# Neighbourhood attention: the values of four head pairs by seven block products, and two small moves in the layer after it

## The reference, cut to what matters

```
def na_mixer(h, hc, w_qkv, rpb, w_o, need_ctx):      # h: latent tokens, hc: context tokens, 256 each
    q = project_q(h)                                 # h @ w_qkv[:, :1024]
    k, v = project_kv(h)                             # h @ w_qkv[:, 1024:]
    kc, vc = project_kv(hc)
    y = neighbourhood_attention(q, k, v, kc, vc, rpb).reshape(B, S, H * d) @ w_o
```

## Time and profile before

| | |
|---|---|
| median of three runs | 1903.69 us (1902.11 to 1905.91) |
| profiled execution | 1905.67 us, span 1903.8 us |
| TensorE busy (PE) | 1743.9 us, 92% of the span; granted clock 0.969 in the mean |
| VectorE busy (DVE) | 915.2 us, 48% |
| ScalarE busy (ACT) | 367.5 us, 19% |
| DMA | 395.77 MB, mean 208 GB/s |
| chain that ended last | PE 78%, DMA 18%, DVE 3% |

### The profile page before, as it was taken

The page is one execution under the profiler, slowest core; times in us unless marked ns, Lnnn a source line. Parts: engine busy times, 40 slices in busy tenths (PEclk is TensorE's granted clock), DMA queues, the critical chain, the costliest instruction groups (busy, mean ns, idle before and its releaser), DMA issues.

```text
span 1903.8 us, 33559 instructions
## 1 busy us (share of the span) xinstructions
PE 1743.9 (92%) x14306; PEld 1374.2 (72%) x14306; DVE 915.2 (48%) x1948; ACT 367.5 (19%) x872; POOL 0.2 (0%) x4
## 2 busy tenths in 40 slices
PE   8999999999999999999999999999999866666765
PEld 4455687888888886777888888788888655445554
DVE  1488878666666426677544412478433211111112
ACT  0343413221110114222211102203412100000001
POOL 0000000000000000000000000000000000000000
PEclk9999999999999999999999999999999988888888
DMA  9523342222222116445243533313296999999997
GB/s 382 205 112 143 125 177 89 89 84 82 82 100 95 65 61 219 165 165 196 91 169 140 222 153 133 133 67 133 89 377 249 426 428 429 428 429 428 429 427 298
DMA packets 32947, 395.77 MB, mean 208 GB/s; under 512 B 3664, under 2 KB 6736, under 8 KB 9040
## 3 DMA queue, kind: packets, MB, share of 16 engines
q1 hardware_dynamic: 32848, 394.33, 51.8%
HBM read 393.26 MB, written 1.05 MB: 207 GB/s over the span
## 4 chain that ended last, share of the span: by engine, by line
PE 78%; DMA 18%; DVE 3%; issue 1%; ACT 1%; SPq 0%; DVEq 0%
PE bank L600 24%; PE bank L1880 13%; DMA arena<-w_moe 10%; PE bank L1589 8%; DMA ring<-w_moe 7%; PE bank L653 5%; PE bank L3349 3%; PE bank L2093 3%; PE bank L898 2%; PE bank L2089 1%; PE bank L1199 1%; PE bank L807 1%; PE bank L2449 1%; PE bank L1175 1%; PE bank L3360 1%; PE bank L2145 1%
## 5 line engine op out<-in xcount | busy, mean ns | idle before, releaser
L600 PE MATMUL bank<-layer_input,ring 128*128 128x256 f32 x1152 | 255.3, 382 | 0.0
L600 PEld LDWEIGHTS bank<-layer_input,ring 128*128 128x128 f32 x1152 | 219.2, 192 | 31.9 <-issue 2.6
L3349 PE MATMUL bank<-arena 128*32 128x128 f32 x2008 | 79.8, 325 | 51.6 <-DMA arena<-w_moe 51.4
L1589 PE MATMUL bank<-arena,ring 128*128 128x256 f32 x544 | 121.8, 380 | 0.5 <-DMA ring<-w_ffn_out 0.5
L3501 DVE TENSOR_TENSOR arena<-arena,bank 128x128 f32<-128x128 f32 x32 | 9.2, 287 | 223.0 <-PE bank L3349 223.0
L1880 PE MATMUL bank<-arena 128*128 128x256 f32 x504 | 115.7, 379 | 0.0
L3349 PEld LDWEIGHTS bank<-arena 128*32 128x32 f32 x2008 | 69.1, 131 | 63.0 <-DMA arena<-w_moe 61.2
L1589 PEld LDWEIGHTS bank<-arena,ring 128*128 128x128 f32 x544 | 103.2, 190 | 15.1 <-DMA ring<-w_ffn_out 0.9
L1880 PEld LDWEIGHTS bank<-arena 128*128 128x128 f32 x504 | 95.8, 190 | 13.0 <-DVE arena L2009 0.2
L653 PE MATMUL bank<-arena,ring 128*128 128x256 f32 x452 | 99.1, 380 | 0.8 <-DVE arena L2252 0.6
L653 PEld LDWEIGHTS bank<-arena,ring 128*128 128x128 f32 x452 | 85.7, 190 | 13.2 <-issue 1.0
(11 more groups left out here) (505 smaller groups left out, 2667.4 us busy)
## 6 DMA issues: line engine op xcount, KB each, us to landing
arena<-w_moe SPq DMA_DIRECT2D x45, 2048.0 KB, 25.8
ring<-w_moe SPq DMA_DIRECT2D x45, 2048.0 KB, 26.5
ring<-w_ffn_in SPq DMA_DIRECT2D x22, 2048.0 KB, 7.7
ring<-w_ffn_out SPq DMA_DIRECT2D x8, 2816.0 KB, 9.9
ring<-w_proj SPq DMA_DIRECT2D x7, 3072.0 KB, 9.9
ring<-w_ada_late SPq DMA_DIRECT2D x8, 2560.0 KB, 9.0
ring<-w_na_pair SPq DMA_DIRECT2D x8, 1536.0 KB, 6.2
arena<-w_far SPq DMA_DIRECT2D x11, 1024.0 KB, 6.7
```

What stands on the lines that cost most here:

```text
L600: last = pe.matmul(out, a, b, start=(k == 0), stop=(k == len(lhs) - 1))
L1589: last = eng.matmul(out, w[:, k * P:(k + 1) * P], x[:, k, :], start=(start and k == 0), stop=(stop and k == half - 1), skip_group_check=True)
L3349: ins = eng.matmul(bank[x][group[q], 0:P], xe[:, k, SLOTS * e:SLOTS * e + SLOTS], weight(e, first, last, (x * KT + k) * FE + q * P, P), st ...
```

## The change

**Values by seven products.** The values of four pairs are made at once, in two groups (g = 0 for pairs 0 to 3, g = 1 for pairs 4 to 7). For a group the tokens (halved into context and latent) times the weights (channels halved, output columns halved) are a 2 x 2 block product. It is computed by seven block products in place of eight, in the form with sums made beforehand: four sums of token halves (`s1` to `s4`, once, for both groups), four of weight halves (`t1` to `t4`, per group, in the ring's own slot), all made by VectorE with one operation of 128 x 1024 each. A block product for one half i of 128 tokens is four matmuls of 128 x 128 weights with 256 columns; there are 7 x 2 x 2 = 28 of them. ScalarE takes five intermediate results per (g, i) out of PSUM (`snap`, 128 x 256), and VectorE adds three per (g, i) (`cross`, two; `far_right`, one).

**Stream.** The pairs' chunks are six of 2048 KB: queries and keys of pairs 0 and 1, values of group 0, queries and keys of 2 and 3, values of group 1, queries and keys of 4 and 5, and of 6 and 7. The biases are kept for 8 heads at a time, and those of heads 8 to 15 are loaded in two parts during turns 1 and 3. The far tiles come one by one (512 KB) into two buffers, 32 loads.

```diff
-FAR_BUFFERS, FAR_EACH = 3, 2
-FAR_PER_PAIR = (0, 4, 4, 4, 5, 5, 5, 5)
+FAR_BUFFERS, FAR_EACH = 2, 1
+FAR_PER_PAIR = (8, 1, 5, 6, 6, 3, 3, 0)
...
-          ("na_pair", NA_PAIRS, 3072), ("na_o", 2, 4096),
+          ("na_pair", 6, 4096), ("na_o", 2, 4096),
...
         i, used = FAR_BUFFERS, 0
+        values_done = {0: VALUE_STEPS, 4: 2 * VALUE_STEPS}
         for u in range(NA_PAIRS):
-            if u + RING < NA_PAIRS:
-                sp.wait_ge(self.sem("na_proj_done"), u + 1)
-                load(u + RING, (g0 + u) % 2, g0 + u + RING)
+            if u == 0:
+                sp.wait_ge(self.sem("na_qk_done"), 4)
+                load(2, g0 % 2, g0 + 2)
+            if u in (1, 3):
+                sp.wait_ge(self.sem("na_biased"), 8 if u == 1 else 16)
+                heads = slice(0, 4) if u == 1 else slice(4, 8)
+                self.load_biases(sp, 8, heads, self.rest_in)
             used += FAR_PER_PAIR[u]
-            while i < min(FAR_LOADS, used // FAR_EACH + FAR_BUFFERS):
+            while i < min(FAR_LOADS, used):
                 self.load_far(sp, i)
                 i += 1
+            if u in values_done:
+                sp.wait_ge(self.sem("products_done"), NA_VALUES["products_done"] + values_done[u])
+                load(3 if u == 0 else 5, (g0 + 1) % 2, g0 + (3 if u == 0 else 5))
+            if u == 2:
+                sp.wait_ge(self.sem("na_qk_done"), 8)
+                load(4, g0 % 2, g0 + 4)
+            while i < min(FAR_LOADS, used + FAR_BUFFERS):
+                self.load_far(sp, i)
+                i += 1
...
-        sp.wait_ge(self.phase_done, self.merged)
+        sp.wait_ge(self.mixed, KT)
...
+        def value(g, i, n):
+            w, at = self.na_value_weights(g), self.na_steps(g, i)
+            near, far = slice(i * P, i * P + P), slice(CTX + i * P, CTX + i * P + P)
+            low, high, far_high = self.A[:, 0:4, near], self.A[:, 4:8, near], self.A[:, 4:8, far]
+            s1, s2, s3, s4 = [x[:, :, near] for x in v["sums"]]
+            x, y, out, start = {1: (low, "lo0", left, True), 2: (high, "hi0", first_cross, True),
+                                3: (s1, "t1", second_cross, True), 4: (s2, "t2", left, False),
+                                5: (s4, "hi1", second_cross, False), 6: (s3, "t3", left, False),
+                                7: (far_high, "t4", left, False)}[n]
+            if (i, n) == (0, 1):
+                self.na_value_loaded(pe, g)
+            if n in (3, 4, 5, 6, 7):
+                pe.wait_ge(s["vector_in"], ready + ((0, 0, 0, 2, 4, 6, 7, 8), (0, 0, 0, 9, 10, 10, 11, 12))[g][n])
+            if n == 1 and (g, i) != (0, 0):
+                pe.wait_ge(s["scalar_out"], at["free"])
+            if n == 2 and (g, i) != (0, 0):
+                pe.wait_ge(s["vector_out"], at["pair_free"])
+            if n in (4, 5, 6, 7):
+                pe.wait_ge(s["scalar_out"], at[{4: "first", 5: "fifth", 6: "second", 7: "third"}[n]])
+            for k in range(4):
+                last = pe.matmul(out, x[:, k, :], w[y][:, k * CTX:(k + 1) * CTX], start=(start and k == 0), stop=(k == 3),
+                                 skip_group_check=True)
+            last.then_inc(s["products_done"], 1)
...
+        def weight_sum(g, n, count):
+            w = self.na_value_weights(g)
+            if n == 1:
+                self.na_value_loaded(dve, g)
+            if n == 4:
+                dve.wait_ge(s["products_done"], self.na_value_done(g, 1, 2))
+            x, y = {1: ("lo1", "lo0"), 2: ("hi1", "t1"), 3: ("hi1", "lo1"), 4: ("hi0", "t2")}[n]
+            add(w[f"t{n}"], w[x], w[y], ALU.subtract, count)
+        def cross(g, i):
+            at, home = self.na_steps(g, i), self.na_value_homes(v, g, i)
+            dve.wait_ge(s["products_done"], self.na_value_done(g, i, 5))
+            dve.wait_ge(s["scalar_out"], at["second"])
+            if g == 1:
+                dve.wait_ge(s["o_done"], 2)
+            dve.tensor_tensor(home["c11"], bank[7][:, 0:CTX], v["first"], ALU.add).then_inc(s["vector_out"], 1)
+            dve.tensor_tensor(home["c12"], bank[7][:, CTX:2 * CTX], v["second"], ALU.add).then_inc(s["vector_out"], 1)
+        def far_right(g, i):
+            at, home = self.na_steps(g, i), self.na_value_homes(v, g, i)
+            dve.wait_ge(s["scalar_out"], at["third"])
+            dve.tensor_tensor(home["c22"], v["third"], v["fifth"], ALU.add).then_inc(s["vector_out"], 1)
...
         dve.wait_ge(s["squared"], at["squared"] + KT)
-        dve.memset(v["blk"], 0.0).then_inc(s["cmp_steps"], 1)
...
-        for n in range(6):
+        for n in range(4):
+            evict(n)
+        dve.memset(v["blk"], 0.0).then_inc(s["cmp_steps"], 1)
+        for n in (4, 5):
             evict(n)
...
-        self.phase_end(eng, who)
...
-            link(dve.tensor_tensor(mixed[:, oc, :], mixed[:, oc, :], other, ALU.add))
+            dve.tensor_tensor(mixed[:, oc, :], mixed[:, oc, :], other, ALU.add).then_inc(self.mixed, 1)
...
+            if oc == 0:
+                pe.wait_ge(self.sem("branch_used"), KT - 1)
+            for k in range(KT):
+                if oc == 0:
+                    pe.wait_ge(self.mixed, k + 1)
+                w = ((oc % 4) * KT + k) * P
+                last = pe.matmul(bank[oc % 2][:, 0:LAT], self.w_out_chunk(oc // 4)[:, w:w + P], mixed[:, k, :],
+                                 start=(k == 0), stop=(k == KT - 1))
+            last.then_inc(s["y_ready"], 1)
```

More of the change, by code:

```diff
@@ new lines, in queries @@
+        def queries(u, lo=0, hi=KT):
+            if lo == 0:
+                pe.wait_ge(s["q_copied"], u)
+            for k in range(lo, hi):
+                last = query(u, k)
+            if hi == KT:
+                last.then_inc(s["qk_done"], 1)
+        left, first_cross, second_cross = bank[2][:, 0:CTX], bank[7][:, 0:CTX], bank[7][:, CTX:2 * CTX]
+        ready = NA_VALUES["vector_in"]
+        def value(g, i, n):
[21 more added lines that the diff above has]
+            last.then_inc(s["products_done"], 1)
@@ new lines, in na_heads_dve, with add @@
+        ready_0 = NA_VALUES["vector_in"]
+        A = [[self.A[:, 4 * y:4 * y + 4, c:c + CTX] for y in range(2)] for c in (0, CTX)]
+        s1, s2, s3, s4 = v["sums"]
+        def add(out, x, y, op, count):
+            dve.tensor_tensor(out, x, y, op).then_inc(ready, 1)
+            dve.wait_ge(ready, ready_0 + count)
+        def weight_sum(g, n, count):
[6 more added lines that the diff above has]
+            add(w[f"t{n}"], w[x], w[y], ALU.subtract, count)
@@ new lines, in na_heads_dve @@
+        maxima(0)
+        weight_sum(0, 3, 5)
+        add(s4, A[0][1], s2, ALU.subtract, 6)
+        add(s3, A[0][0], A[1][0], ALU.subtract, 7)
+        normalize(0)
+        cross(0, 0)
+        fars(0, 0, 1)
+        queries(1)
+        weight_sum(0, 4, 8)
+        fars(0, 1, 2)
+        turned(0)
+        far_right(0, 0)
+        fars(0, 2, 4)
+        cross(0, 1)
+        fars(0, 4, 6)
+        far_right(0, 1)
+        fars(0, 6, 8)
+        attended(0)
+        maxima(1)
+        weight_sum(1, 1, 9)
@@ new lines, in na_heads_dve @@
+        normalize(1)
+        weight_sum(1, 2, 10)
+        turned(1)
+        weight_sum(1, 3, 11)
+        queries(2)
+        fars(1, 0, 1)
+        attended(1)
+        maxima(2)
+        normalize(2)
+        cross(1, 0)
+        fars(2, 0, 2)
+        turned(2)
+        fars(2, 2, 3)
+        queries(3)
+        weight_sum(1, 4, 12)
+        fars(2, 3, 5)
+        attended(2)
+        maxima(3)
+        normalize(3)
+        fars(3, 0, 3)
+        turned(3)
+        far_right(1, 0)
+        fars(3, 3, 4)
@@ L2242, in na_heads_dve @@
+        queries(4)
+        fars(3, 4, 6)
+        attended(3)
+        maxima(4)
+        normalize(4)
+        cross(1, 1)
+        fars(4, 0, 3)
+        turned(4)
+        far_right(1, 1)
+        fars(4, 3, 4)
+        queries(5)
+        fars(4, 4, 6)
+        attended(4)
+        for u in (5, 6):
             maxima(u)
             normalize(u)
-            for i in range(min(FAR_PER_PAIR[u], 4)):
-                far(sum(FAR_PER_PAIR[:u]) + i)
-            self.na_turned(u, 0, s, v, dve, dve.tensor_copy, "pt_dve")
@@ L2247, in na_heads_dve @@
-            if FAR_PER_PAIR[u] > 4:
-                far(sum(FAR_PER_PAIR[:u]) + 4)
-            if u + 1 < NA_PAIRS:
-                queries(u + 1)
-            dve.wait_ge(s["o_done"], u + 1)
-            dve.tensor_copy(v["oT"][:, u * LAT:(u + 1) * LAT], bank[6][:, 0:LAT]).then_inc(s["o_used"], 1)
+            fars(u, 0, 2)
+            turned(u)
+            fars(u, 2, 3)
+            queries(u + 1)
+            attended(u)
+        maxima(7)
+        normalize(7)
+        turned(7)
+        attended(7)
```

289 lines of the change are left out of this document (206 added, 83 removed).

## The result

| | before | after |
|---|---|---|
| median | 1902.9 us (4 runs) | 1911.07 us (4 runs, 1909.52 to 1912.65) |
| ratio | | 1.0038, 95% interval 1.0026 to 1.005 |
| profiled execution | 1905.67 us, span 1903.8 | 1909.74 us, span 1908.0 |
| TensorE / VectorE busy | 1743.9 / 915.2 us | 1740.3 / 933.3 us |
| last copy of the attention output | 907.60 | 919.14 |

The changed kernel is slower by about 0.4%. The forecast was 1905.2 with a range of 1896.0 to 1911.5: the time lies at the upper end of the range, and the size is nearer to that of rival (b), two far buffers as the bound, than to the forecast.

What follows compares the result with a forecast made beforehand. TensorE was taken to bound the kernel up to the experts, DMA among them. Attention +3.9, clearing -1.0 and merge -1.4 gave +1.5 us: 1907.2 against the profiled execution, 1905.2 against the median of 1903.69; range 1896 to 1911.5.

Steps and rivals of the forecast that it cites:

- rival (b): Attention stage: two far buffers set the pace; at 4.5 us per load instead of 3.5, +9.1 us, 1912.8; chance 0.25.
- TensorE relieved by 10.3 us: Values in the attention stage: 28 block products of 1.73 us, 48.4 us, replace 58.7 us of TensorE work.
- rival (c): Values: 256-column records run at the pace of two of 128, a product takes 1.83 us; +2.2 on the forecast, 1907.4; chance 0.05.
- Turn 0 without a wait: First attention turn: VectorE's sums come in time for TensorE's products, `s4` at 740.8, wanted at 741.7, cover 0.9 us.
- Two buffers late for the far tiles: Turns 2 to 4: end of a tile to start of the one after next takes 3.5 us, tiles 0.9 to 3.5 late.
- The chunks behind far loads: Key chunks for turns 4 and 5 and pairs 6 and 7 queue behind far loads 13 and 25, issued 807.9 and 857.9.
- the walk: Turn-by-turn estimate of the attention stage's output copies, from 789.9 in turn 1 to the last at 911.5, 3.9 us later than before.
- TensorE could begin `keys(4)` at 813.1 and waits 2.9: Turn 3: the keys' chunk lands at 816, so TensorE waits 2.9 us, then keys take 6.87.
- Turn 1: VectorE, copy to copy, takes 16.9 us, including 0.5 for ScalarE's snapshot ahead of the exponentials; TensorE's list is 15.9.
- The last turn: End of the attention stage: attention ends 14.4 us after the previous copy instead of 19.1; output weights may be 1.5 late.
- Clearing and merge: Second block: moving the `memset` from ahead of the sums gains 1.0 us, projection starting directly behind the branches gains 1.4.
- Its point of decision, 3.8 us: Rival (b): the kernel is slower by over 3.8 us from a far load of 3.8 us on.

Runs made afterwards that it cites:

- the version with the filler: Changed kernel with four single far buffers, plus eight 128x128 products of constants ahead of the last turn's transposes: 1900.41 us, ratio 0.998 to the kernel before.
- The fillers: Changed kernel with unused products of constants where TensorE stood in turns 3 and 5, two far buffers kept: 1908.3 us, ratio 1.0022 to the kernel before.

## Why the prediction was right in direction and short in size

The forecast had the change 1.5 us slower, and by the medians it is 8.2. The range held the result, but in part by luck: its upper end had been drawn for loads of up to 4.3 us, and what came instead was a clock that fell and two smaller terms.

**TensorE relieved by 10.3 us: right.** Products come every 1.73 us (738.16 to 743.34 for three, in the version with the filler), so rival (c) falls.

**Turn 0 without a wait: right,** 57.8 against 57.7 us.

**Two buffers late for the far tiles: right, and a little under.** From the end of a tile to the start of the one after next it is 3.64 and 3.90 us in turn 2 and 3.89 in turn 4 (3.6 to 3.9 in the seven waits of turns 2 to 6), of which the load itself is 3.47, for the first, and 3.72, for the third; I took 3.5 in all. So the landing was at most 0.4 us over the middle value, well under the 4.5 us of rival (b). Turn 2's miss of 0.6 us is this. The Trainium skill ("DMA: Bandwidth & Descriptors", Anatomy of one DMA) would give an estimate of 3.2 for the load; the measured ones are above it. The fit there is measured on transfers that GpSimd issues, which the prediction did not say, and these are issued on SyncE.

**The chunks behind far loads: right.** Issued at 809.1 and 862.6, landed 8.25 and 8.56 us later; the walk had 807.9 and 857.9, and 8.1 and 7.9. With four buffers both waits shrink to 1.06 and 0.28.

**What the waits cost: wrong, and this is the main miss.** The step "TensorE could begin `keys(4)` at 813.1 and waits 2.9" took a wait to cost its own length and the work after it 6.87 us. The work after it ran at half the clock: 2.8 us more in turn 3, 1.5 in turn 5. The fillers show it. Of the 8.1 us by which the stage missed its forecast 4.4 stand in these two rows, and 3.3 came back at the stage's end when the fillers took them away.

**Turn 1: 1.3 us short, by ScalarE.** Turn 1 is 18.2 us with two buffers and with four, and with the far tiles halved, so it is neither loads nor far tiles. The walk had counted 0.5 for ScalarE's snapshot ahead of the exponentials. The rows show more (the first two of the changed kernel, the last of the kernel before):

```profile
780.04 0.37 ACT L2528 COPY extra<-bank 128x256 f32<-128x256 f32 x1 [8.64 <-PE bank L2187]
780.43 1.28 ACT L2515 ACT_TABLE_LOAD   x1
...
746.86 1.28 ACT L2275 ACT_TABLE_LOAD   x1
```

The snapshot waits for TensorE's product until 780.04, 0.4 us after the negated maximum is there, and behind it stands a table load, which ScalarE makes before the first exponential after the silu. In the kernel before it stood directly behind the silu, nine microseconds before the exponentials of turn 1 could start, and cost nothing. Now the exponentials start at 781.73 instead of 779.7, and TensorE waits 0.69 and 0.25 for probabilities and 0.44 for a sum. No run here moved that load, so this is read from the rows and not tested.

**The other turns.** Some 1.8 us are left over the other turns, 0.8 of it in turn 5, where the chunk took 8.56 us to land for the walk's 7.9.

**The last turn: right,** 14.6 us against 14.4, with the output weights 1.52 us late under its hole.

**Clearing and merge: near.** Forecast 1.0 and 1.4. The clearing is worth 1.1 between two traces that both keep the clock (212.5 and 211.5, before rounding), the merge 1.7. The 3.2 beyond, in the profile of before, are the clock again.

**The balance.** Stage +12.0, clearing -4.3, merge -1.7, the start and the stretches without a change -1.8: +4.2 in span, +4.1 of time in the two profiled executions (1905.67 and 1909.74). The medians are 8.2 apart, since before's profiled execution lay 2.8 above its median and after's 1.3 below its own.

**Rival (b) against the forecast.** Its copies (814.3, 840.9, 868.2, 886.5, 904.7, 919.1) are within 1.2 us of the measured ones, but for another reason: it put 4.5 us from the end of a tile to the start of the one after next, and they took 3.6 to 3.9, with the clock and the table load in the place of the difference. Its point of decision, 3.8 us, was just reached. By its own numbers, 7.6 us of time for one of load, 3.9 us would have made 3 us over the forecast (an estimate), where the stage had 8.1.

## What to carry to other kernels

Price a new wait of the bound engine as the wait and what the clock does after it: read the granted clock behind holes of the kernel that you have, there may be one of the same size. Before moving work to an engine with slack, look at what else hangs on the same order: here two buffers put the far loads, the keys' chunk and TensorE's next turn in one chain, and two more buffers brought back 10 of 12 us. A gain on one engine shows only when every turn has room for it; the next 5 us (0.9987 to 0.9962) came from a filler in the last turn's hole and from moving single operations to the turns and engines that waited. And when an operation goes ahead of exponentials, look at what ScalarE has to load in front of them.

## What I had not expected of the hardware

- The granted clock went from 1.00 to 0.50 after TensorE had worked 2.39 of 6 us (811 to 817) and stayed there until about 823; in the last turn of the version with four buffers it fell after a standstill of 1.99 us, with the records before it dense; at the head of before's mixer it fell with TensorE at 1.43 and 1.18 of 2 us. Products of constants in the hole kept it at 1.00 each time that they were tried (turns 3, 5 and 7).
- It is not the same in every execution. With the same mixer code one trace had 1.18 us of work from 1194 to 1196 and a clock of 0.66, another 1.36 and 1.00; the stretch took 3.2 us more in the first. A difference of this size between two single traces is no effect of an edit by itself.
- Not every hole costs it. In the changed kernel's last turn TensorE worked 1.18, 0.81 and 1.68 of 2 us from 904 to 910, and the clock stayed at 1.00. What tells this from 811 to 817 the runs here leave open. Nor is the length of the wait what tells them apart: with the tiles moved by turn the keys of turn 3 took 7.13 us after a wait of 2.21, and with the filler in the last turn added, the same code up to there, 8.83 after one of 1.78.
